# Sparse attention in a one-core decoder layer: sixteen row blocks of a third as one chain, with the value products and the weight and mix splits at other places in it

## What is computed

```python
qg = q.reshape(B, S, G, R, hd).transpose(0, 2, 3, 1, 4) * hd ** -0.5      # G=2 groups, R=3 heads each
c_logits = einsum('bgrsd,bgcd->bgrsc', qg, k_cmp) + c_bias                # 31 compressed blocks
o_cmp = einsum('bgrsc,bgcd->bgrsd', masked_softmax(c_logits, c_mask), v_cmp)
p = masked_softmax(einsum('bgrqd,bgqkd->bgrqk', qb, kg) + bias, mask)     # selected blocks: at 512 tokens all
o_slc = einsum('bgrqk,bgqkd->bgrqd', p, vg)
p = masked_softmax(einsum('bgrqd,bgkd->bgrqk', qb, kb) + w_bias, mask)    # window of 512
o_win = einsum('bgrqk,bgkd->bgrqd', p, vb)
o = gates[0] * o_cmp + gates[1] * o_slc + gates[2] * o_win
```

## Time and profile before

| what | value |
|---|---|
| time, median of 3 (lowest to highest) | 2722.93 us (2722.27 to 2723.21) |
| the profiled execution: its time, its span | 2723.4 us, 2721.6 us |
| PE busy | 2581.6 us, 95% of the span, 11880 matmuls |
| DVE busy, ACT busy | 1398.9 us (51%), 859.5 us (32%) |
| granted TensorE clock, mean | 0.98 of full speed |
| memory traffic | 251.78 MB, mean 93 GB/s |

### The profile page before, as it was taken

How to read it: one execution, slowest core, us unless ns; L and a number is a source line. 1 busy time by engine, 2 the same in 40 slices (tenths; PEclk the granted TensorE clock), 3 DMA queues, 4 the chain that set the end, 5 groups by cost and what they waited for, 6 DMA issues and landing times.

```text
span 2721.6 us, 33363 instructions
## 1 busy us (share of the span) xinstructions
PE 2581.6 (95%) x11880; PEld 2098.2 (77%) x11880; DVE 1398.9 (51%) x2313; ACT 859.5 (32%) x1578; POOL 55.7 (2%) x42
## 2 busy tenths in 40 slices
PE   7899999989999887999999999999999999999996
PEld 5777877767788554788888888888888888888884
DVE  4776666634344555336444454444444544444446
ACT  4433233323223434224323232222222232323232
POOL 0110011100000000000000000000000000000000
PEclk9999999999999997999999999999999999999998
DMA  4311111121325002422232222322222222222222
GB/s 159 140 47 51 66 56 60 35 101 66 120 93 211 14 35 77 177 93 95 94 108 93 92 94 91 108 92 95 106 92 92 94 91 108 94 106 93 92 93 77
DMA packets 41593, 251.78 MB, mean 93 GB/s; under 512 B 5392, under 2 KB 5648, under 8 KB 13884
## 3 DMA queue, kind: packets, MB, share of 16 engines
q1 hardware_dynamic: 41532, 250.96, 25.6%
HBM read 243.04 MB, written 13.15 MB: 94 GB/s over the span
## 4 chain that ended last, share of the span: by engine, by line
PE 53%; DVE 1%; ACT 0%; issue 0%; DVEq 0%; ACTq 0%
PE bank L231 35%; PE bank L1588 17%; DVE x_t L1737 0%; DVE head_out L1668 0%; ACT head_out L1711 0%; DVE rms_row L1734 0%; PE bank L1690 0%; DVE x_t L1660 0%; PE bank L1575 0%; ACT rms_row L1713 0%; DVEq L1550 0%; ACTq L1710 0%; DVEq L1717 0%
## 5 line engine op out<-in xcount | busy, mean ns | idle before, releaser
L231 PE MATMUL bank<-h_hi,w_hi 128*128 128x512 f32 x2176 | 887.5, 408 | 36.9 <-DVE w_lo L191 32.0
L231 PE MATMUL bank<-h_lo,w_hi 128*128 128x512 f32 x2176 | 855.4, 393 | 0.0
L231 PE MATMUL bank<-h_hi,w_lo 128*128 128x512 f32 x2176 | 854.9, 393 | 0.0
L231 PEld LDWEIGHTS bank<-h_hi,w_hi 128*128 128x128 f32 x2176 | 414.1, 190 | 129.3 <-DVE w_lo L191 19.4
L231 PEld LDWEIGHTS bank<-h_lo,w_hi 128*128 128x128 f32 x2176 | 412.8, 190 | 89.1
L231 PEld LDWEIGHTS bank<-h_hi,w_lo 128*128 128x128 f32 x2176 | 414.3, 190 | 84.5 <-issue 4.8
L182 ACT ACTIVATE w_hi<-w_raw_far 128x512 fp32r<-128x512 f32 x528 | 307.1, 624 | 439.4 <-PE bank L1588 274.8
L191 DVE TENSOR_TENSOR w_lo<-w_raw_far,w_hi 128x512 fp32r<-128x512 f32 x528 | 331.2, 687 | 123.8 <-ACT w_hi L182 122.5
L191 DVE TENSOR_TENSOR w_lo<-w_raw,w_hi 128x512 fp32r<-128x512 f32 x312 | 215.8, 735 | 202.8 <-ACT w_hi L182 202.5
L1588 PE MATMUL bank<-h_hi,w_hi 128*128 128x512 f32 x704 | 274.4, 390 | 1.0 <-DVE x_t L1660 1.0
L1588 PE MATMUL bank<-h_hi,w_lo 128*128 128x512 f32 x704 | 273.9, 389 | 0.0
(11 more groups left out here) (283 smaller groups left out, 1982.1 us busy)
## 6 DMA issues: line engine op xcount, KB each, us to landing
w_raw_far<-in_weights SPq DMA_DIRECT2D x132, 1024.0 KB, 4.7
w_raw<-in_weights SPq DMA_DIRECT2D x77, 1024.0 KB, 4.8
x_t<-in_x_t SPq DMA_DIRECT2D x7, 1024.0 KB, 9.9
bias_rows<-bias_row SPq DMA_DIRECT2D x10, 512.0 KB, 7.1
out<-x_t SPq DMA_DIRECT2D x8, 512.0 KB, 2.7
mix_scratch<-head_out SPq DMA_DIRECT2D x14, 256.0 KB
nsa_tab<-bias_rows SPq DMA_DIRECT2D x6, 448.0 KB, 7.3
h_lo<-mix_scratch SPq DMA_DIRECT2D x1, 2560.0 KB, 12.0
```

What stands on the lines that cost most here:

```text
L231: m = nc.tensor.matmul(PB[pb][:], a[:, s, k], b, start=(kt == 0 and n == 0), stop=(kt == KT - 1 and n == 2))
```

## The change

PE's loop over four attentions becomes one loop over 16 steps `t` = 4i + b. A step first makes the scores of `t+2`, then does its filler steps (1 and 2 by turns; in the last third none in the first seven steps and then 2 each), then, at `b` = 0, the value products of the attention before, and last the turn of `t`. The scores of steps 0 and 1 are made early in the third, as soon as `c_m` is raised, ahead of the 8 filler steps. ACT does in step `t` the exponential of `t`, the eviction of `t-1`, and then a mix split (last third, from `t` = 4) or, in odd steps, one weight split. DVE does the rows of `t`, the scaling of `t-1`, then the low part of the same split. The number of splits, fillers and products is as before.

```diff
@@ PE, nsa_pe
-            NSA_FILLS = (2, 1, 0, 0), (2, 2, 2, 1), (2, 2, 2, 1), (2, 2, 2, KT)
-            WO_FILLS = (0, 0, 0, 0), (0, 0, 0, 2), (2, 2, 2, 2), (2, 2, 2, KT)
+            STEPS = 4 * TB
+            NSA_FILLS = (1, 2) * (STEPS // 2)
+            WO_FILLS = (0,) * 7 + (2,) * 9
...
+                for t in range(2):
+                    pe.wait_ge(c_m, 2 * r + t + 1)
+                    step_scores(t)
                 fill(0 if last else 8)
                 for g in range(NSA_G):
                     pe.wait_ge(c_p, 2 * r + g + 1)
...
-                n0 = N4 + 4 * r
-                scores(n0, 0, qs[0], kT[0][0])
-                scores(n0, 1, qs[0], kT[0][0])
...
-                for i, (g, br) in enumerate(seq):
-                    nxt = seq[i + 1] if i < 3 else None
-                    attend_pe(pe, n0 + i, kT[br][g], qs[g], vt[br][g], lg, PT, PB[2 + g], False, br == 1, fill,
-                              (WO_FILLS if last else NSA_FILLS)[i],
-                              None if nxt is None else (qs[nxt[0]], kT[nxt[1]][nxt[0]]))
+                for t in range(STEPS):
+                    i, b = t // TB, t % TB
+                    if t + 2 < STEPS:
+                        pe.wait_ge(att_m, 4 * (n0 + i) + b + 1)
+                        step_scores(t + 2)
+                    fill((WO_FILLS if last else NSA_FILLS)[t])
+                    if b == 0 and i > 0:
+                        values(i - 1)
+                    if t >= 2:
+                        pe.wait_ge(att_pt, 4 * n0 + t - 1)
+                    pe.wait_ge(att_p, 4 * (n0 + i) + b + 1)
+                    for sb_ in range(b + 1):
+                        m = nc.tensor.transpose(W[2 + b % 2][:, sb_ * P:(sb_ + 1) * P], lg[:, b, sb_ * P:(sb_ + 1) * P],
+                                                ident)
+                    m.then_inc(att_t, 1)
+                fill(1000)
+                values(3)
@@ ACT, nsa_act
+                exps(0)
                 if not last:
                     sp_hi(1)
...
-                for i in range(4):
-                    attend_act(act, N4 + 4 * r + i, lg, nm, den, PT, i == 0,
-                               (lambda k: mix_step(mix_hi, act)) if last and i else lambda k: None)
-                    if not last:
-                        sp_hi(2)
+                for t in range(STEPS):
+                    if t:
+                        exps(t)
+                        turned(t - 1)
+                    if last and t >= TB:
+                        mix_step(mix_hi, act)
+                    if not last and t % 2:
+                        sp_hi(1)
+                turned(STEPS - 1)
@@ DVE, nsa_dve
+                rows(0)
                 if not last:
                     sp_lo(1)
...
-                for i in range(4):
-                    g, br = i // 2, i % 2
-                    attend_dve(dve, N4 + 4 * r + i, lg, nm, den, bias_of(g), gs[:, 3 * g + 1 + br, :], i == 0,
-                               (lambda k: mix_step(mix_lo, dve)) if last and i else lambda k: None)
-                    if not last:
-                        sp_lo(2)
+                for t in range(STEPS):
+                    if t:
+                        rows(t)
+                        norm(t - 1)
+                    if last and t >= TB:
+                        mix_step(mix_lo, dve)
+                    if not last and t % 2:
+                        sp_lo(1)
+                norm(STEPS - 1)
```

More of the change, by code:

```diff
@@ L1159, in nsa_pe, with group, step_scores, values @@
                     m.then_inc(c_s, 1)
+                n0 = N4 + 4 * r
+                def group(i):
+                    return i // 2, i % 2
+                def step_scores(t):
+                    g, br = group(t // TB)
+                    scores(n0 + t // TB, t % TB, qs[g], kT[br][g])
+                def values(i):
+                    g, br = group(i)
+                    pe.wait_ge(att_pt, 4 * (n0 + i) + TB)
+                    for sb_ in range(TB):
+                        m = nc.tensor.matmul(PB[2 + g][:, sb_ * P:SEQ], vt[br][g][:, sb_, :], PT[:, sb_, sb_ * P:SEQ],
+                                             start=False, stop=(br == 1 and sb_ == TB - 1))
+                    m.then_inc(att_o, 1)
+                for t in range(2):
+                    pe.wait_ge(c_m, 2 * r + t + 1)
+                    step_scores(t)
                 fill(0 if last else 8)
@@ L1171, in nsa_pe @@
                     nc.tensor.matmul(PB[2 + g][:], vc[:, g, :], PTc[:, g, :], start=True, stop=False).then_inc(c_o, 1)
-                seq = [(g, br) for g in range(NSA_G) for br in range(2)]
-                for i, (g, br) in enumerate(seq):
-                    nxt = seq[i + 1] if i < 3 else None
-                    attend_pe(pe, n0 + i, kT[br][g], qs[g], vt[br][g], lg, PT, PB[2 + g], False, br == 1, fill,
-                              (WO_FILLS if last else NSA_FILLS)[i],
-                              None if nxt is None else (qs[nxt[0]], kT[nxt[1]][nxt[0]]))
+                for t in range(STEPS):
[15 more added lines that the diff above has]
+                values(3)
             mixed = {mix_hi: 0, mix_lo: 0}
@@ L1203, in nsa_act, with exps, turned @@
                             astep(ins)
+                n0 = N4 + 4 * r
+                def exps(t):
+                    b = t % TB
+                    act.wait_ge(att_m, 4 * n0 + t + 1)
+                    nc.scalar.activation(lg[:, b, 0:(b + 1) * P], lg[:, b, 0:(b + 1) * P], ACT.Exp,
+                                         bias=nm[:, b:b + 1], accum_out=den[:, b:b + 1]).then_inc(att_e, 1)
+                def turned(t):
+                    b = t % TB
+                    act.wait_ge(att_t, 4 * n0 + t + 1)
+                    if b == 0 and t:
+                        act.wait_ge(att_o, n0 + t // TB)
+                    nc.scalar.activation(PT[:, 0:b + 1, b * P:(b + 1) * P],
+                                         W[2 + b % 2][:, 0:(b + 1) * P].rearrange("p (s n) -> p s n", n=P),
+                                         ACT.Copy).then_inc(att_pt, 1)
+                exps(0)
                 if not last:
@@ L1208, in nsa_act @@
                     nc.scalar.activation(PTc[:, g, :], W[2 + g][0:N_CMP, :], ACT.Copy).then_inc(c_pt, 1)
-                for i in range(4):
-                    attend_act(act, N4 + 4 * r + i, lg, nm, den, PT, i == 0,
-                               (lambda k: mix_step(mix_hi, act)) if last and i else lambda k: None)
-                    if not last:
-                        sp_hi(2)
+                for t in range(STEPS):
[7 more added lines that the diff above has]
+                turned(STEPS - 1)
+                if last:
+                    for _ in range(TB):
+                        mix_step(mix_hi, act)
+                sp_hi(8)
                 if last:
@@ L1257, in nsa_dve, with rows, norm @@
                     nc.vector.tensor_scalar(nmc[:, g, :], nmc[:, g, :], BIG / 10, None, ALU.min).then_inc(c_m, 1)
+                n0 = N4 + 4 * r
+                def rows(t):
+                    i, b = t // TB, t % TB
+                    if i:
+                        dve.wait_ge(att_t, 4 * n0 + t - TB + 1)
+                    att_rows(dve, n0 + i, b, lg, nm, bias_of(i // 2))
+                def norm(t):
+                    i, b = t // TB, t % TB
+                    att_norm(dve, n0 + i, b, lg, den, gs[:, 3 * (i // 2) + 1 + i % 2, :])
+                rows(0)
                 if not last:
@@ L1278, in nsa_dve @@
                 else:
+                    sp_lo(8)
                     dve.wait_ge(att_p, 4 * (N4 + 4 * (r + 1)))
```

2 lines of the change are left out of this document (removed).

## The result

The changed kernel took 2726.84 us (median of 20 executions, 2721.29 to 2729.86), the kernel before beside it 2721.26 (20 executions, 2715.52 to 2724.64; the three of the table above were near its upper end). The ratio is 1.0022, 95% interval 1.0015 to 1.0028: slower by 4 to 8 us, on the border of the 0.2% that the prediction called no change. The forecast was 2726.5 with a range of 2716 to 2737.

What follows compares the result with a forecast made beforehand. Only the sparse attention, 200.5 us or 7.4% of the span, could change, bound by waiting for a chain through DVE, PE and ACT. The terms summed to +3.6 against the profiled 2723.4; forecast 2726.5 us, range 2716 to 2737.

Steps and rivals of the forecast that it cites:

- loop, first and second third: Four attentions of each of the first two thirds: 49.2 us a loop, -1.1 and -2.4.
- start, first and second third: Start of a third up to the turn of block 0: 15.3 us (+2.8) in the first, 16.3 (-0.2) in the second.
- last third, start and attention 0: Last third: start gains nothing; attention 0 no longer waits for scores of blocks 2 and 3 behind a turn, -2.4.
- attention 1 (with the part at half clock): Last third: period 15.7 against 14.65, +1.0, plus 0.4 for a part at half clock.
- attention 2, attention 3 to its last turn: Last third: period 15.7 against 12.88, +2.8; turn of 3 at 11.1 against 8.44, +2.7.
- The chain: First two thirds: DVE's next rows wait for scaling, turn, eviction, high split and low split; period 12.87 us.
- The sign named for it: DVE's low split waiting for ACT eight times as long in sum as one 1.90 row.
- Then PE is the limit: Behind the turn of block 3, value products stand ahead of the next turn: 0.43 + 0.64 + 0.68 + 2.13 = 3.88 us.
- The step named: In the starts, PE now waits for the maxima before the 8 filler steps.
- Rival 1: Starts and attention 1 at half clock, from PE's two waits for `c_m`: +10 on the forecast, 2736 us; chance 0.25.
- by the page: Reading of the skill section: new waits for the maxima are paid twice, as a wait and as slow filler behind it.
- Rival 2: Splits don't hold DVE, so the period is PE's 9.5, 3.1 less in each of eight attentions: 2696 us; chance 0.08.

Runs made afterwards that it cites:

- the kernel with late mix splits: The kernel before with only the last third's mix split moved behind the eviction: 2729.11 us, 1.0031 (1.0021 to 1.0042).
- the two traces that stayed at 1.00: The changed kernel with filler steps 0, 2, 2, 2 in place of 1, 2, 1, 2 in the first two thirds, measured twice: 2722.67 and 2722.25 us.
- the kernel with that order changed: The changed kernel with ACT making both weight and mix splits ahead of the eviction instead of behind it: 2695.92 us, 0.9908 of the kernel before.

## Why the prediction was right

The mechanism was right and the change small, as forecast. That the total came out within 0.3 us, 2726.5 against 2726.84, is luck: the change measured 5.6 us where 3.6 was forecast, and the baseline that it was added to, a median of three, was 1.7 too high (2722.93 against 2721.26 over 20 executions). Against the stretches, term by term:

| term | forecast | in the two traces |
|---|---|---|
| loop, first and second third | -1.1, -2.4 | -0.3, -1.6 |
| start, first and second third | +2.8, -0.2 | +3.3, +0.9 |
| last third, start and attention 0 | -2.4 | -5.0 |
| attention 1 (with the part at half clock) | +1.4 | +2.7 |
| attention 2, attention 3 to its last turn | +2.8, +2.7 | +3.1, +2.7 |
| behind it | 0 | +0.5 |
| sum | +3.6 | +6.4 |

- **The chain.** The period was worked out as 12.87 and is 13.04 to 13.11. Step by step, from the turn of block 0: 3.62 (forecast 3.52), 5.53 (5.43), 9.14 (8.99), 13.10 (12.87). The four steps are longer than the forecast by 0.10, 0.00, 0.05 and 0.08, which no term had. That the loops would gain next to nothing because the splits hold DVE was right, and was shown both ways: taken away from the changed kernel, it gave 31 us, and the mix splits' part of it, put alone into the kernel before, cost 8 to 10. The sign named for it, low splits waiting eight times 1.90 = 15.2 us, came out as 17.5. The 1.90 itself was read from one attention: the other three of the kernel before waited 2.6 to 2.8, 10.1 in sum.
- **The border.** "Then PE is the limit" was right for the turn, and slightly off in why: the eviction of block 3 stands hard behind it, and taking the filler step away gave 0.40 of 0.68.
- **The starts.** The step named was right. The first start stood at 15.8 where 15.3 was forecast. In the second third the clock was 0.80, lower than the first start's 0.86 which I had carried over, and the turn stood at 17.4, not 16.3. Which clock a start gets was a guess in both thirds: a second trace of the same kernel has 17.0 (0.80) and 16.15 (0.89), and the kernel before varies too (16.53 at 0.82, and 15.20 at 0.86 in the trace of the kernel with late mix splits, where this part is the same).
- **Rival 1** did not come to pass at its price: no start was under 0.7 but the last third's, 0.67, which was so before too (0.66). Its mechanism, a wait that is paid again as slow filler, is there in part: up to 2.9 us in the second start, by the working above, and nothing of it in the two traces that stayed at 1.00. That these waits would be paid twice "by the page" is more than the section named says: in the Trainium skill, TensorE: Matmul & The Clock Gate, section "HAM oscillation — how this bites in real kernels", the waits last longer than the bursts between them.
- **Rival 2** was given 0.08 because ACT's order excluded it. Its price, 2696, is what the kernel with that order changed took, 2695.9; that this too is so close is partly luck, since the period came down to 10.39 and not to PE's 9.5, and the last third gave 8.7 us up to its last turn where some 5 were priced.
- **The last third, attention 0.** The forecast took its clock to stay at 0.57; it was 0.87, and the attention took 9.4 in place of the 11.5 worked out. But the term was too small at the slow clock as well: in the four kernels where this order had 0.61 or 0.62 it took 10.05 to 10.15, against 13.86 for the order before, at 0.57 and at 0.61. The turn of row block 2 comes 3.8 us earlier there (4.31 against 8.15 us behind that of block 0), where the forecast took off 3.0 for the scores; what the rest is was not followed. Over all ten traces of this order it took 9.0 (0.93) to 10.4 (0.72). The start ahead of it was 0.5 shorter, where nothing was forecast.
- **Attention 1.** Its clock was lower than assumed (0.71), and it cost 1.3 more than forecast. The second trace of the changed kernel has 16.90 at 0.80. Why the clock is granted here and not there was not settled. The errors in attentions 0 and 1 are of opposite sign, -2.6 with the start and +1.3, and those of the loops (+1.6) and the starts (+1.6) stand against the first.

## What to carry to other kernels

An engine that runs in program order ties together whatever stands next to each other in it. A piece of work whose input is there and that has no deadline, such as a weight split here, should stand ahead of the instruction that waits, not behind it, above all when another engine waits for that piece before going on with the critical chain. Before building a deeper pipeline, follow one wait of the slowest engine back across the others: here the deeper order cost 6 us, and gained 25 once one instruction on a third engine, which was idle more than half the time, changed places with its neighbour.

## What was not expected

Three small matters. The steps of the chain came out up to 0.10 us longer than the rows of single instruction pairs of the kernel before suggest, a quarter of a us in each attention, and that is what a forecast of this kind can't resolve. In the trace of the changed kernel the waits for the maxima in the second start last 0.86 and 0.69 us, and the start is 3.5 us longer than without them, because the filler behind them ran at the slow clock: its matmuls follow one another by 0.43 us until 958, by 0.23 after. In other traces the same waits left the clock at 1.00. And executions of one kernel differed by 9 us (2715.52 to 2724.64), more than the change is worth, so that one or three of each could hardly have told it from nothing; 20 beside 20 did, and 8 beside 18 again (1.0024, 1.0014 to 1.0035).
